# Low parts of the down-projection weights: a subtraction on GpSimd becomes an adding transfer from HBM

## The reference, cut to what matters

```
for each of 2 layers:
    u = rms_norm(h) @ w_in                    # 1024 -> 14 column groups
    y = concat(SSD(u), Retention(u), GLA(u), RG_LRU(u))
    h = h + y @ w_out                         # 1024 -> 1024
    n = rms_norm(h)
    h = h + (silu(n @ w_gate) * (n @ w_up)) @ w_down   # 1024 -> 2816 -> 1024
y = rms_norm(h)
```

## Time and profile before

| what | value |
|---|---|
| median of three runs | 1356.48 us |
| profiled execution: time, span | 1357.07 us, 1355.3 us |
| granted TensorE clock, mean | 0.981 of full speed |
| TensorE (PE) busy | 1303.7 us, 96% of the span |
| VectorE (DVE) busy | 855.5 us, 63% |
| ScalarE (ACT) busy | 708.6 us, 52% |
| GpSimd (POOL) busy | 292.2 us, 22% |
| read from HBM | 180.33 MB |
| GpSimd subtractions of 128x1024 | 50, 123.7 us in all |

### The profile page before, as it was taken

The page is one execution under the profiler, slowest core; times in us unless marked ns, Lnnn a source line. Parts: engine busy times, 40 slices in busy tenths (PEclk is TensorE's granted clock), DMA queues, the critical chain, the costliest instruction groups (busy, mean ns, idle before and its releaser), DMA issues.

```text
span 1355.3 us, 26923 instructions
## 1 busy us (share of the span) xinstructions
PE 1303.7 (96%) x10781; PEld 1253.4 (92%) x10781; DVE 855.5 (63%) x1696; ACT 708.6 (52%) x1207; POOL 292.2 (22%) x248
## 2 busy tenths in 40 slices
PE   7999999998999999999999999999899999999996
PEld 7988898988999999999998888899799999999996
DVE  5844765577853785378657546656688358834854
ACT  7625355556642664266563264656576246624641
POOL 1100101112242224224411010101123412341250
PEclk9999999998999999999999999999899999999998
DMA  8755645646753775376466476457377347734741
GB/s 275 201 116 142 154 109 117 140 99 149 171 150 84 164 171 145 84 166 167 132 151 155 110 160 143 94 114 173 82 164 186 111 102 164 186 109 102 169 120 66
DMA packets 63387, 189.73 MB, mean 140 GB/s; under 512 B 7584, under 2 KB 8864, under 8 KB 63264
## 3 DMA queue, kind: packets, MB, share of 16 engines
q0 software_dynamic: 27936, 67.12, 29.9%
q1 hardware_dynamic: 30672, 111.95, 26.0%
q10 hardware_dynamic: 4656, 8.95, 2.1%
HBM read 180.33 MB, written 5.43 MB: 137 GB/s over the span
## 4 chain that ended last, share of the span: by engine, by line
PE 78%; DVE 11%; ACT 5%; DVEq 3%; issue 2%; DMA 1%; ACTq 0%
PE bank L1586 39%; PE bank L1615 30%; DVE ct L949 1%; PE bank L1529 1%; DVE up L1463 1%; ACT wh L537 1%; DVE lru_x L949 1%; DMA raw<-weights 1%; DVEq L1441 1%; DVE tz L1459 1%; ACT wl L536 1%; PE bank L1903 1%; PE bank L1547 0%; PE bank L1909 0%; DVE xl L904 0%
## 5 line engine op out<-in xcount | busy, mean ns | idle before, releaser
L508 POOL DMA_DIRECT2D wl<-weights x194 | 168.3, 867 | 913.9 <-ACT wl L536 912.4
L1586 PE MATMUL bank<-xh,wh 128*128 128x272 f32 x800 | 243.9, 305 | 8.0 <-DVE xl L904 7.7
L537 ACT ACTIVATE wh<-raw 128x512 fp32r<-128x512 f32 (+1 forms) x243 | 198.3, 816 | 94.7 <-PE bank L1586 83.1
L1586 PE MATMUL bank<-xh,wl 128*128 128x272 f32 x800 | 235.3, 294 | 0.0
L1586 PE MATMUL bank<-xl,wh 128*128 128x272 f32 x800 | 234.3, 293 | 0.0
L536 ACT ACTIVATE wl<-raw 128x512 fp32r<-128x512 f32 (+1 forms) x194 | 147.1, 758 | 128.0 <-PE bank L1586 116.1
L1615 PE MATMUL bank<-xh,wh 128*128 128x272 f32 x704 | 204.6, 291 | 0.0
L1615 PE MATMUL bank<-xh,wl 128*128 128x272 f32 x704 | 204.5, 290 | 0.0
L1615 PE MATMUL bank<-xl,wh 128*128 128x272 f32 x704 | 204.0, 290 | 0.0
L537 ACT ACTIVATE wh<-wsum 128x512 fp32r<-128x512 f32 x176 | 105.8, 623 | 146.3 <-DVE wsum L1366 107.0
L1615 PE MATMUL bank<-sxh,wh 128*128 128x272 f32 x528 | 155.1, 294 | 19.5 <-ACT u L799 19.2
(11 more groups left out here) (401 smaller groups left out, 3018.1 us busy)
## 6 DMA issues: line engine op xcount, KB each, us to landing
raw<-weights SPq DMA_DIRECT2D x202, 512.0 KB, 6.2
wl<-weights POOLq DMA_DIRECT2D x132, 256.0 KB, 5.3
wl<-weights POOLq DMA_DIRECT2D x62, 512.0 KB, 7.2
h<-x SPq DMA_DIRECT2D x4, 544.0 KB, 6.0
y<-h SPq DMA_DIRECT2D x4, 544.0 KB, 2.7
rv<-rk ACTq DMA_DIRECT2D x8, 136.0 KB, 2.7
tz<-rq ACTq DMA_DIRECT2D x8, 136.0 KB, 5.5
S<-s_ssd ACTq DMA_DIRECT2D x2, 512.0 KB, 6.0
```

Of the source, the lines that this page charges most:

```text
L508: nc.gpsimd.dma_start(wl[:, place(j)], weights[n][:, lo:lo + width], accum_op=ALU.add).then_inc(lo_added[BLOCK0[j] % RING], 16)
L537: a(wh[:, place(j)], whole, ACT.Copy).then_inc(hi_done, 1)
L1586: ins = mm(bank_, wt[:, at:at + P], xx[:, cols], start=(i == 0 and pass_ == 0), stop=(i == len(ks) - 1 and pass_ == 2))
```

## The change

One function changes. The 24 down units of each layer, 48 in all, go from `ON_POOL` to `FROM_HBM`. Output units (25 to 32) were `FROM_HBM` already, and unit 2 of layer 0 and unit 0 of layer 1 stay on GpSimd, units 0 and 1 of layer 0 on VectorE.

```diff
     if kind == "unit":
         if (layer, i) in ((0, 0), (0, 1)):
             return ON_VECTOR
-        return FROM_HBM if (3 if layer == 0 else 1) <= i < FFN0 else ON_POOL
+        if (layer, i) in ((0, 2), (1, 0)):
+            return ON_POOL
+        return FROM_HBM
     return {"P1": FROM_HBM, "P2": FROM_HBM, "P3": FROM_HBM, "P4": ON_VECTOR, "P5": ON_VECTOR, "P6": ON_VECTOR,
             "P7": ON_VECTOR}[kind]
```

## The result

The changed kernel takes 1385.57 us (median of four runs, 1384.97 to 1389.14) beside 1357.56 us for the kernel before on the same chip: a ratio of 1.0209, interval 1.0185 to 1.0233. That is 28 us slower. The profiled execution took 1385.93 us, with a span of 1384.1 us, 28.8 us over that of before.

What follows compares the result with a forecast made beforehand. TensorE, busy 1303.7 of 1355.3 us, was taken as the bound. Stalls of 18.8 less a gain of 3.0 gave +15.8 us on 1357.07: 1372.9 profiled, 1372.3 us as median of the runs, range 1367 to 1386.

Steps and rivals of the forecast that it cites:

- that PEclk falls after the stalls: Sign of a wrong forecast: TensorE's granted clock drops behind the new waits at first down units.
- What bounds the kernel: Whole kernel: TensorE busy 1303.7 of 1355.3 us, waiting nowhere directly for GpSimd's subtractions; removing 48 is by itself worth 0.
- The gain of 3.0 us: End of each layer's last group: VectorE's stretched operations shorten, TensorE's two waits for gl_gla go; 2 x 1.48 us.
- The hidden additions: Down units: ScalarE's 48 copies (50.5 us) and GpSimd's 48 issues (0.867 us each) stay hidden, price 0.
- The added wait: First down unit of six groups: TensorE waits for the adding transfer, 3.2 us each (2.3 to 5.0), 18.8 us in all.
- L - 4.42 us: TensorE's stall at a group's first down unit; L is issue to landing, taken as 7.6 us (6.7 to 9.4).
- The clock: TensorE's granted clock behind the 3.2 us stalls: counted as held, price 0; if not, 6 x 2.7 = 16 us more.
- rival C: Transfers become the bound (1399 us), or TensorE's clock falls after the stalls (16 us more, 1388 us); chance 0.08.
- A (in time): Group ends: low parts land in under 4.42 us, no stall, only VectorE's relief, 1353.5 us; chance 0.12.
- B: First down units: landing between 4.42 and 6.7 us, half a stall, +3.6 us, 1360 us; chance 0.08.
- C's first half: Down units: DMA queue builds up, first units land only after 12.0 us, stalls 45 us, 1399 us; chance 0.08 with clock case.
- The other down units: Down units after each group's first: low parts land in time; unit 1, next in danger, about even without the stall.

Runs made afterwards that it cites:

- the third experiment: Kernel before, but down units 1 to 3 of each layer's last group (six in all) by adding transfers; 1354.91 us, ratio 0.9977.
- the copying version: Changed kernel, but the 48 down-unit transfers copy instead of adding; 1374.73 us, ratio 1.0129.
- the first experiment: Changed kernel, but the first down unit of each of the six groups is subtracted on GpSimd again; 1355.04 us, ratio 0.9979.
- the version in halves: Changed kernel, but each group's first down unit is negated and added in two 256 KB halves, each with its own semaphore; 1374.57 us, ratio 1.0107.
- low pass last: Changed kernel, but down unit 0's first piece does its wl passes last, waiting for the landing only before them; 1370.40 us, ratio 1.0108.

## Why the prediction was right

The place, the number and the cause of the new waits were right, and the time, 1385.57 us, lies in the range of 1367 to 1386. But it lies 0.4 us under its upper end, and that is luck. The upper end stood for landings of 9.4 us at all six places and no gain; the landings were 8.1 us and the gain came. What filled the range was the clock, which the sum had at 0. The forecast proper was 15.8 us more, and 28.8 were measured in the profiled execution. One of the signs that the prediction named for being wrong, that PEclk falls after the stalls, did show.

**What bounds the kernel: held.** TensorE waited nowhere for a subtraction, and taking 48 of them away gave only what they did to VectorE.

**The gain of 3.0 us: held.** L1463 (now L1465) and L1459 (now L1461) are at 0.73 us, the two waits for gl_gla are gone, and ScalarE's additional copy did not eat the gain. Shown alone by the third experiment. Most of it would have come with the six first units alone, which left 0.7 us of gl_gla's 3.0.

**The hidden additions: held.** ScalarE's additional copies and GpSimd's issues appear in no wait of TensorE's first down units beyond the 1.06 us counted in the sum. The waits for `take_u2` grew from 19.2 to 20.2 us through one more wait in layer 1's first group; it is 0.8 us in the copying version and 0.5 us in the first experiment. Just before it VectorE waits for a raw load, 1.77, 1.59 and 1.05 us in these three against 0.58 us before; why that load came later was not tried. The wait of 1.1 us in the P stage has nothing of the change before it and appears again only in the version in halves (1.3 us), so it goes with the execution and not with the change.

**The added wait: held in place and number, a little small in size.** The step was "L - 4.42 us" at each of six places. I took L as 7.6 us; it was 8.1 on average, between my bounds, with 0.25 us more until TensorE starts, for which the sum had nothing: 22.6 us of stalls for 18.8. The rows that I took L from, whole units of the input stage, share the DMA engines less, which I saw and priced too low. The copying version and the one with the later raw load show two parts: about 1.4 us of the 8.1 are the adding at this place, 1.7 are the raw loads that follow. SyncE's earlier loads stood in the prediction at 0 because TensorE waits for none of them; that they share the DMA engines with the new transfer was not priced.

**The clock: the wrong term.** The prediction put it at 0 because behind 1.8 us of idle time it had held, and kept 16 us for it under rival C. That row is one of two: the same trace has the same wait in layer 0, 1.75 us long, and there the clock fell.

```profile
128.78 0.44 PE L1828 MATMUL bank<-sq_sum,V 128*64 128x128 f32 x4 [1.75 <-ACT K L639]
```

```profile
130.20:133.40 3.20, 3.20 (x16) 0.50 0.98 233
```

(The second fence: stretch, TensorE busy (matmuls), PEclk, DMA share, GB/s.) So the rows of before gave no ground for a price of 0 behind 3.2 us. In the changed kernel it fell behind five stalls of 3.4 to 4.4 us and cost 6.9 us, 1.4 each and not 2.7: the stretch at half speed was 3 us long, not 6. With L this is most of the difference between the +15.8 us forecast and the +28.8 us of the profiled execution: 3.8 us of stalls, 6.9 of clock, and 2.3 in the small waits of the P stage and for `take_u2`, whose cause is open.

**The rivals.** A (in time) fell, all six landings being 7.1 us or longer; B fell with it. C's first half, transfers as the bound, fell with the first experiment; its second half, the clock, came true at under half its price. The other down units were in time behind the stalls, as forecast.

## What to carry to other kernels

When an operand's producer is exchanged for one with a longer latency, the average cover says nothing: list the lead of each use, from the freeing of its buffer to its first read, and look for the shortest. Here 40 of 48 uses had enough of it, two were short of 0.8 us, and the six with the shortest lead cost nearly everything; doing the exchange only where the old producer disturbed somebody (six other uses) kept the gain. A stall of a dense TensorE can have a second price in its clock. Here each stall of 3.1 us and more paid it, about 1.4 us in the changed kernel, and some shorter ones did; a single row in which the clock held is no ground for a price of 0. And where the profile names an odd releaser for a wait on several semaphores, hold its end against the landing of the transfer.

## What the runs showed of the hardware

- An adding DMA of 512 KB took 7.0 us to land where the same copy took 3.9 us (medians of 24 each: 7.2 and 4.0 us). GpSimd's issue mostly took 862 ns in the one and 527 ns in the other.
- Holding the next raw load (and so those behind it) back until the adding transfer had landed took 1.7 us off its landing (8.1 to 6.4 us on average).
- Of the stalls of TensorE at first down units, over all these runs, the clock fell behind each of the thirteen of 3.1 us and more. Of those between 1.9 and 3.0 us it fell behind three (1.97, 2.66 and 2.94 us) and held behind nine (1.93 to 2.98 us). Of two stalls of 2.66 us, it fell behind the one (in halves) and held behind the other (low pass last): the length of the stall alone does not decide it.
- VectorE's 128x544 operation on two SBUF operands took 0.73 us alone and up to 2.8 us when it started during a GpSimd subtraction, ending about 0.58 us after it; when it started first, it took 0.73 us and the subtraction up to 2.9 instead of 2.4 us.
